# Products into an unread PSUM bank at the border of two stages, and four bonus rows placed inside a projection

## The reference, cut to what matters

```python
h = rms_norm(x, norm_mix)
p = h @ w_in                                    # 1024 x 2816, 22 blocks of 128 columns
...
rh, kh, vh, ah = heads(r), heads(k), heads(v), heads(a)
y, s_new = wkv7_scan(wkv0, rh, heads(decay), kh, vh, kk, kk * ah)
...
bonus = jnp.sum(rh * kh * r_k, axis=-1, keepdims=True) * vh
y = (y + bonus.reshape(*bonus.shape[:-2], C_A)) * g
return y, s_new, p_a[:, -1]                     # the last projected row is an output
...
x = x + jnp.concatenate([y_a, y_b], axis=-1) @ w_out
x = x + moe_ffn(rms_norm(x, norm_ffn), ...)     # top 4 of 32 experts
```

## Time and profile before

| what | value |
|---|---|
| median of 3 runs | 1227.79 us (1225.31 to 1228.66) |
| the profiled execution's own time | 1228.13 us |
| its span, first to last instruction | 1226.2 us |
| mean granted PE clock | 0.992 of full speed |
| PE busy | 1191.6 us (97%) |
| DVE / ACT / POOL busy | 453.1 / 198.9 / 30.7 us |
| stage one, border, scan and output projection, experts | 0 to 139.0, 139.0 to 140.2, 140.2 to about 296, about 296 to 1226.2 us |

### The profile page before, as it was taken

One profiled execution on the slowest core, in us unless ns is written; L12 is line 12 of the kernel. 1 busy time (PEld: TensorE's weight loads), 2 busy tenths in 40 slices (PEclk: granted clock), 3 DMA queues, 4 the chain that ended last, 5 costly groups with the idle time before them and its releaser, 6 DMA issues.

```text
span 1226.2 us, 19111 instructions
## 1 busy us (share of the span) xinstructions
PE 1191.6 (97%) x8032; PEld 540.3 (44%) x8032; DVE 453.1 (37%) x993; ACT 198.9 (16%) x437; POOL 30.7 (3%) x34
## 2 busy tenths in 40 slices
PE   8999999999999999999999999999999999999995
PEld 6676799854333333333333333333333333333332
DVE  6899442253523332222232233332222222222224
ACT  4345223124100110010010000100001000001002
POOL 0000050030000000000000000000000000000000
PEclk9999998999999999999999999999999999999998
DMA  9521121388999999999999999999999999999993
GB/s 261 177 69 47 44 73 38 88 362 311 425 427 427 428 428 426 428 430 428 428 429 428 429 428 428 430 430 428 428 429 428 429 428 428 430 429 428 427 427 153
DMA packets 53596, 430.25 MB, mean 351 GB/s; under 512 B 12175, under 2 KB 25919, under 8 KB 28702
## 3 DMA queue, kind: packets, MB, share of 16 engines
q1 hardware_dynamic: 53314, 428.91, 84.9%
q10 hardware_dynamic: 228, 0.55, 0.1%
HBM read 424.92 MB, written 4.48 MB: 350 GB/s over the span
## 4 chain that ended last, share of the span: by engine, by line
PE 67%; DMA 19%; DVE 1%; ACT 1%; issue 0%; POOL 0%; DVEq 0%
PE bank L1830 41%; DMA ring<-in_w_up_dram 19%; PE bank L1808 6%; PE bank L1884 5%; PE bank L1087 3%; PE bank L1815 2%; PE bank L1163 2%; PE bank L1437 2%; PE bank L1759 1%; PE bank L1043 1%; PE bank L1838 1%; PE bank L1068 1%; PE bank L1856 1%; PE bank L1136 0%; PE bank L1216 0%; PE bank L1212 0%
## 5 line engine op out<-in xcount | busy, mean ns | idle before, releaser
L1830 PE MATMUL bank<-ring,arena 128*64 128x512 f32 x1536 | 342.3, 594 | 7.5 <-DMA ring<-in_w_up_dram 6.8
L1830 PE MATMUL bank<-arena 128*64 128x512 f32 x1536 | 342.6, 594 | 6.0 <-DMA arena<-in_w_up_dram 6.0
L1830 PEld LDWEIGHTS bank<-ring,arena 128*64 128x64 f32 x1536 | 109.3, 137 | 218.7 <-issue 200.7
L1830 PEld LDWEIGHTS bank<-arena 128*64 128x64 f32 x1536 | 109.2, 136 | 216.6 <-issue 199.1
L2105 DVE TENSOR_SCALAR arena<-bank 128x512 f32<-128x512 f32 x32 | 22.1, 692 | 380.2 <-PE bank L1838 380.2
L2119 DVE TENSOR_TENSOR arena<-arena,bank 128x512 f32<-128x512 f32 x186 | 113.6, 679 | 1.5 <-PE bank L1884 1.5
L535 PE MATMUL bank<-arena,ring 128*128 128x336 f32 x352 | 102.5, 447 | 0.3 <-ACT arena L352 0.3
L1884 PE MATMUL bank<-arena 64*128 64x512 f32 (+1 forms) x384 | 91.1, 606 | 0.7 <-issue 0.7
L1808 PE MATMUL bank<-arena 128*64 128x512 f32 (+1 forms) x384 | 89.6, 600 | 0.1
L2109 DVE TENSOR_SCALAR arena<-bank 128x512 f32<-128x512 f32 x32 | 22.1, 692 | 176.4 <-PE bank L1838 176.4
L535 PEld LDWEIGHTS bank<-arena,ring 128*128 128x128 f32 x352 | 66.0, 190 | 33.6 <-issue 2.0
(11 more groups left out here) (357 smaller groups left out, 790.6 us busy)
## 6 DMA issues: line engine op xcount, KB each, us to landing
ring<-in_w_gate_dram SPq DMA_DIRECT2D x32, 2048.0 KB, 24.4
arena<-in_w_up_dram SPq DMA_DIRECT2D x32, 2048.0 KB, 27.4
ring<-in_w_down_dram SPq DMA_DIRECT2D x32, 2048.0 KB, 30.9
arena<-in_w_gate_dram SPq DMA_DIRECT2D x32, 2048.0 KB, 26.1
ring<-in_w_up_dram SPq DMA_DIRECT2D x32, 2048.0 KB, 28.6
arena<-in_w_down_dram SPq DMA_DIRECT2D x31, 2048.0 KB, 30.5
ring<-in_w_in_dram SPq DMA_DIRECT2D x11, 1024.0 KB, 8.1
ring<-in_w_out_dram SPq DMA_DIRECT2D x4, 1024.0 KB, 5.0
```

The source lines that it names most:

```text
L1830: mm = M.matmul(bank[64 * hb:64 * hb + 64, b, :], tokens(cc), w[:, c, 512 * hb:512 * hb + 512], start=(cc == 0), stop=(w3 == 2 and cc == K ...
```

## The change

Three edits. First, the bonus rows (`head_rows` of `rksum`) no longer follow the last block but stand inside it, between its fourth and its fifth product; on ACT their four copies now stand ahead of `evacuate(21)`. Second, products of `ones` with itself into columns 384 to 511 of bank 3, which nobody reads, are added in two places of stage one: four between the last block and the wait for its evacuation, and eight behind the transposition of the last rows, so directly ahead of the barrier. Third, four products of the same kind, into columns 0 to 127 of bank 7, stand ahead of the scan's first turn; the bank is overwritten later.

```diff
@@ ACT, end of stage one
-                evacuate(21)
                 for j in range(4):
                     act.wait_ge(R["rk_sum"], j + 1)
                     A.copy(bonT[:, j, :], bank[:, 4 + j, 0:NT]).then_inc(R["rk_read"], 1)
+                evacuate(21)
@@ PE, project
-                def project(n):
+                def project(n, between=None):
@@
+                        if between and c == 4:
+                            between()
                         mm = M.matmul(bank[:, n % 4, 0:NT], w[:, c, b * P:b * P + P], hT[:, c, :],
@@ PE, end of stage one
-                project(21)
-                pe.wait_ge(R["rk_added_read"], 1)
-                pe.wait_ge(R["s0_read"], 4)
-                head_rows(rksum, "rk_sum")
+
+                def bonus_rows():
+                    pe.wait_ge(R["rk_added_read"], 1)
+                    pe.wait_ge(R["s0_read"], 4)
+                    head_rows(rksum, "rk_sum")
+
+                project(21, bonus_rows)
+                for _ in range(4):
+                    M.matmul(bank[:, 3, 384:512], ones, ones, start=True, stop=True)
                 pe.wait_ge(R["proj_read"], by_scalar(21))
                 M.transpose(bank[0:NBA * (1 + NSEQ), 2, 0:P], lastc[:, :], ident).then_inc(R["last_turned"], 1)
+                for _ in range(8):
+                    M.matmul(bank[:, 3, 384:512], ones, ones, start=True, stop=True)
@@ PE, start of the scan
+            for _ in range(4):
+                M.matmul(bank[:, 7, 0:P], ones, ones, start=True, stop=True)
             for p in range(NP3):
                 turn(3 + p, p, [(vT, CH[2 * p]), (vT, CH[2 * p + 1])]).then_inc(S["v_turned"], 1)
```

## The result

| | before | changed |
|---|---|---|
| median of the 9 runs taken together | 1225.99 us (1223.27 to 1229.16) | 1230.87 us (1228.43 to 1231.29) |
| ratio | | 1.0032, 95% interval 1.0018 to 1.0045 |
| span of the profiled execution | 1226.2 us | 1229.2 us |

The changed kernel is slower by 0.3%, about 3.9 us. The range held the time; the size of the change did not come out as forecast (+0.9 us).

The account below looks back on a forecast made before the run. The end was taken to be set by the expert weight stream, whose start hangs on PE from the border on. Added delay 2.57 less clock gain 1.70 gave +0.9 us: 1227.79 + 0.9 = 1228.7 us, range 1225.4 to 1231.4 us.

Parts of the forecast that it names:

- What bounds the kernel: PE between 131 and 244 us: a microsecond there moves the expert weight stream and the end by about a microsecond.
- The move of the rows and ACT's copies: End of stage one: block ends 0.71 us later, copies leave ACT's tail; the two cancel, ACT 0.06 us earlier.
- The four products ahead of the transposition: Stage one, while PE waits for ACT's evacuation: eight records, 1.0 us, hidden, costing nothing.
- The eight products and the barrier: Behind the transposition: 2.0 us unhidden; PE becomes last at the barrier, 1.57 us later than ACT was before.
- Rival A: At the barrier: it does not wait for the eight products, or they are nearly free; 1227.1 us, chance 0.15.
- The four ahead of the turns: Start of the scan: eight records, 1.0 us, in front of everything; first turn 2.57 us later in all.
- I take it that the clock does not fall: Behind the border: PE's shorter pause of about 1.2 us keeps full clock, gaining 1.70 us; called the least certain step.
- rival B: The clock falls all the same, during or behind the border; the 1.70 us are not won, 1230.4 us, chance 0.20.
- a sign for this: Prediction is wrong if first turn to first expert load differs by more than 1.70 us for a non-border reason.
- C: Border: clock already down when the added products run, costing 3.1 us more; 1231.8 us, slower by over 0.3%, chance 0.07.
- D: Later slow stretches, 190 to 200 and near 240 us, go as well; 1223.6 us, faster by over 0.3%, chance 0.05.
- what I have not thought of: Chance of 0.06 left over for unnamed cases, half within 0.3% to each side and half beyond.

Follow-up runs that it names:

- hidden_only: Kernel before with the bonus rows and ACT's copies moved and only the four products ahead of the transposition added; median 1226.91 us, ratio 1.0001.
- no_eight: Changed kernel without the eight products ahead of the barrier; median 1228.06 us, ratio 0.9999 against the kernel before.
- eight_only: Kernel before with only the eight products ahead of the barrier added; median 1227.79 us, ratio 1.0012.
- the early load: Last quarter of `w_out` loaded in stage one, not the scan: changed kernel 1227.37 us (ratio 0.9999), kernel before 1226.77 us (0.9990).
- scan4_only: Kernel before with only the four products ahead of the first turn added; median 1228.36 us, ratio 1.0016.
- rows_only: Kernel before with only the bonus rows and ACT's copies moved, no product added; median 1227.09 us, ratio 1.0001.
- sixteen: Changed kernel with sixteen products in place of the eight ahead of the barrier; median 1232.36 us, ratio 1.0054 against the kernel before.

## Why the prediction was right or wrong

**What bounds the kernel: right.** From the first wait for ACT in the chunks to the second half of the output projection all profiles take 40.97 or 40.98 us where the third place is not slow and 42.60 to 42.66 where it is, and what PE lost before showed at the end. One reading ahead of it was off: the page's clock is under full speed in one early slice and in the last, not in two early places; nothing hangs on it.

**The move of the rows and ACT's copies: right in effect.** They cancel to within 0.2 us. The block was 0.9 to 1.0 us later and not 0.71; the nearest row had one seam and this interruption has two.

**The four products ahead of the transposition: right.** Free; 0.30 us of waiting were left.

**The eight products and the barrier: right.** The term was +1.57 us; with the late block it measures 1.48 over hidden_only. Rival A is out: PE's end and not ACT's starts the 1.20 us in every profile with eight or more.

**The four ahead of the turns: right.** 1.06 us, forecast 1.0. Together with the rest 2.72 us at the first turn, forecast 2.57.

**"I take it that the clock does not fall", the gain of 1.70 us: right at the border, wrong as a term of the sum.** In five profiles without a product behind the transposition or in front of it the clock fell at the border each time, for 3.4 or 6.8 us. In the nine with some it never did. That is worth 1.5 us or more to the 160 turns, and rival B is out in all of these profiles. But the mean clock over the runs rose only from 0.9931 to 0.9936, worth some 0.5 us at 1 us for 0.001, where no_eight and eight_only with the same clean border reached 0.9943 and 0.9942. The sum charged one stretch and kept the others as they were. It should have counted the whole scan's clock.

**The missing term: the scan behind the border.** The prediction had nothing between the turns and the stream. PE stands there on issue, for 1.17 and 1.03 us in the two profiles of the changed kernel and 0.25 and 0 in those of the kernel before. The sixteen products are 64 instructions more for PE, which moves everything behind them against its instruction packets; that this, together with the load of `w_out` at 185 us, makes the idle time is the explanation that fits, and it is argued and not shown. The idle time stands directly ahead of the small products at which the clock falls. The account against the mean of before is then +2.7 for the border, -0.5 for the clock and +1.0 for issue, 3.2 of the 3.5 us measured (of 4.1 to 4.2 against the runs beside its own). At equal clock 2.7 and 1.0 stand against 4.0. The prediction had named a sign for this: the time from the first turn to the first expert load should shrink by the 1.70 us of the border's clock. It grew from 109.05 to 109.26 us, 1.9 more than forecast, most of it for reasons other than the border: 0.87 us in the scan, 0.85 on SP's queue (not passed on), and only the rest because the border's clock gave 1.52. The strongest evidence is the early load: it is worth 3.1 us to the changed kernel and 0.7 to the one before. Between the two versions with the early load, timed on one chip, the difference is 1227.7 - 1226.5 = +1.1 us, 1.4 either way, where the forecast was +0.9. Its two parts are near the forecast as well: 3.1 us at equal clock, where the sum had 2.57, and a clock that is up from 0.9933 to 0.9952, worth 1.9, where it had 1.70. So with this load out of the scan the runs agree with the prediction's sum, within a wide interval; what it lacked is what goes with the load.

Of the 3.1 us that the early load gives back to the changed kernel about half, 1.6 us, goes with the mean clock (0.9936 to 0.9952), and 1.4 are left at equal clock. Whether the idle time brings the clock down is not shown, nor whether it is the number of added instructions or their place that counts, since neither was varied with the time held fixed. And no_eight is only 0.4 us above before in the mean with the load in place, so the load alone is not the cause.

**Rivals C and D.** C did not occur: the added products ran at full clock except in scan4_only, which has none ahead of the barrier. D's mechanism, that the later stretches come and go, is real, and the kernel before scatters with its mean clock, from 1221.6 to 1232.5 us. But it comes and goes in both kernels: in the profiles of before the stretch near 195 us is 6.8 and 3.4 us, in those of the changed kernel 6.8 and 3.4 as well. With this the rule quoted from the Trainium skill ("TensorE: Matmul & The Clock Gate", "Part 1: The HAM clock gate") agrees. With nothing else at work the time would have risen by the 0.9 us of the sum, and it rose by 3.5 to 4.2.

**The chances.** Slower by over 0.3% had 0.09, and by the ratio the measured 1.0032 and 1.0036 are just that, while by the time, 1230.87 us, it fell within the range, 0.5 us under its upper end. That the range held is partly luck: it reached so high for rival B, which did not occur. The slowdown came by neither C nor D, but by what stood under "what I have not thought of".

## What to carry to other kernels

Products that keep PE's clock up are free only where another engine is the last to arrive. Behind the last real work and ahead of a barrier each is paid in full, so fill PE up to that engine's end and no further. Where a clock's stretches come and go, one profile is one draw: look at the mean clock of all runs, and count the whole stretch of small products and not the place of the edit. And a load that has another place to go is worth trying outside a stretch that is dense in instructions: here that gave 3.1 us to one kernel and 0.7, within noise, to the other.

## What was not expected of the hardware

- PE's clock fell to half behind or within a pause of 2.34 us at the border in four of four profiles, and in rows_only behind pauses of 1.20 and 1.51 us with one transposition between. It stayed up behind 1.51 us in hidden_only and no_eight, where four products stood ahead of the transposition.
- It also fell with PE busy throughout: near 195 us, at products of 64 x 16 and 64 x 64, for 6.8 us in one execution of the kernel before and for 3.4 in another.
- In a stream of 64 x 64 products PE stood still for up to 1.17 us at a time without a semaphore to wait for. Instruction packets are seen on queue q8, and beside a load of 1 MB they came up to 5.6 us apart, without it at most 4.4 in the same stretch. That PE ran out of instructions is the reading that fits.
- The two barriers took 1.20 us from the last engine's end to PE's first instruction, whether ACT (before, rows_only) or PE (after, eight_only, sixteen) came last.
